# Column sums of modulation rows moved within their tiles, and identity products in two waits of TensorE at the start of the local attention

## The reference

```python
c_act = jax.nn.silu(c)
for layer in range(DEPTH):
    mod = c_act @ ada_w[layer] + ada_b[layer]
    shift, scale, gate = jnp.split(mod, 3, axis=-1)
    h = rms_norm(x, norm_w[layer]) * (1.0 + scale[:, None, :]) + shift[:, None, :]
    ...
    x = x + gate[:, None, :] * y
```

```python
sc = jnp.einsum('bnqkgd,bnskd->bnkgqs', qb, kb).astype(jnp.float32) * scale + bias
m = jnp.maximum(jnp.max(sc, axis=-1, keepdims=True), sink_l)
p = jnp.exp(sc - m)
denom = jnp.sum(p, axis=-1, keepdims=True) + jnp.exp(sink_l - m)
o = jnp.einsum('bnkgqs,bnskd->bnqkgd', (p / denom).astype(v.dtype), vb)
```

## Time and profile before

| | us |
|---|---|
| median of 3 runs | 2405.64 (2405.22 to 2407.04) |
| profiled execution: its own time | 2409.29 |
| profiled execution: span from first to last instruction | 2408.0 |
| TensorE busy | 2321.7 |
| VectorE busy | 1395.4 |
| ScalarE busy | 1133.0 |
| GpSimd busy | 929.6 |

### The profile page before, as it was taken

How to read it: one execution, slowest core, us unless ns; L and a number is a source line. 1 busy time by engine, 2 the same in 40 slices (tenths; PEclk the granted TensorE clock), 3 DMA queues, 4 the chain that set the end, 5 groups by cost and what they waited for, 6 DMA issues and landing times.

```text
span 2408.0 us, 31494 instructions
## 1 busy us (share of the span) xinstructions
PE 2321.7 (96%) x12074; PEld 1925.0 (80%) x12074; DVE 1395.4 (58%) x1899; ACT 1133.0 (47%) x1796; POOL 929.6 (39%) x711
## 2 busy tenths in 40 slices
PE   5999999999999999999999999999999999999998
PEld 5888789878888888876678868788877888888887
DVE  6255599768884320139973743332776666666665
ACT  5322388778883221249952474232333333333334
POOL 1111256447642212335521122112265555555551
PEclk9999999999999999999999999999999999999999
DMA  8255300010003221100031221121211111111111
GB/s 307 76 158 168 93 6 1 4 34 1 1 1 123 87 74 44 53 1 1 10 106 44 77 79 44 36 96 53 71 35 53 53 53 53 53 53 53 53 53 70
DMA packets 154091, 146.48 MB, mean 61 GB/s; under 512 B 12295, under 2 KB 141365, under 8 KB 152021
## 3 DMA queue, kind: packets, MB, share of 16 engines
q1 hardware_dynamic: 153940, 144.45, 19.3%
HBM read 123.85 MB, written 16.78 MB: 58 GB/s over the span
## 4 chain that ended last, share of the span: by engine, by line
PE 81%; ACT 6%; DVE 5%; issue 5%; POOL 2%; DMA 1%; SPq 0%; ACTq 0%; DVEq 0%; POOLq 0%
PE ps L256 36%; PE ps L2650 15%; PE ps L2667 9%; PE ps L1126 5%; PE ps L1149 4%; PE ps L1136 4%; ACT C_PR L1807 1%; PE ps L1696 1%; DMA MKW<-in_ada_w 1%; POOL WSL L2567 1%; ACT B_PR L1210 1%; PE ps L1675 1%; PE ps L2626 1%; ACT B_PTH L1204 1%; PE ps L1662 1%
## 5 line engine op out<-in xcount | busy, mean ns | idle before, releaser
L243 POOL TENSOR_TENSOR WL<-WR,WH 128x1024 fp32r<-128x1024 f32 (+2 forms) x87 | 203.6, 2341 | 766.1 <-ACT WH L238 765.9
L256 PE MATMUL ps<-HH,WH 128*128 128x512 f32 (+2 forms) x1136 | 358.8, 397 | 0.0
L256 PE MATMUL ps<-HL,WH 128*128 128x512 f32 (+2 forms) x1136 | 352.1, 391 | 0.0
L256 PE MATMUL ps<-HH,WL 128*128 128x512 f32 x1104 | 341.3, 391 | 0.0
L256 PEld LDWEIGHTS ps<-HL,WH 128*128 128x128 f32 (+2 forms) x1136 | 212.4, 187 | 47.8
L256 PEld LDWEIGHTS ps<-HH,WH 128*128 128x128 f32 (+2 forms) x1136 | 208.3, 187 | 46.7 <-issue 4.1
L256 PEld LDWEIGHTS ps<-HH,WL 128*128 128x128 f32 x1104 | 208.2, 189 | 44.0
L2880 DVE TENSOR_TENSOR XF<-ps,XF 128x1024 f32<-128x1024 f32 x168 | 201.5, 1220 | 32.7 <-PE ps L2667 26.1
L2650 PE MATMUL ps<-HC,WSH 128*128 128x512 f32 x640 | 197.0, 389 | 0.0
L1162 DVE TENSOR_REDUCE NM<-ps 128x1 f32<-128x1024 f32 x128 | 156.5, 1223 | 33.5 <-PE ps L1126 32.0
L2567 POOL TENSOR_TENSOR WSL<-WSR,WSH 128x512 fp32r<-128x512 f32 x100 | 131.5, 1315 | 107.6 <-ACT WSH L2561 107.6
(11 more groups left out here) (433 smaller groups left out, 5183.0 us busy)
## 6 DMA issues: line engine op xcount, KB each, us to landing
WS<-in_w_ffn_in SPq DMA_DIRECT2D x44, 512.0 KB, 5.0
MKW<-in_ada_w SPq DMA_DIRECT2D x32, 512.0 KB, 4.3
spill<-X SPq DMA_DIRECT2D x3, 4096.0 KB, 13.6
OW<-in_w_ffn_out SPq DMA_DIRECT2D x22, 512.0 KB, 3.5
WR<-in_odd_w_in SPq DMA_DIRECT2D x19, 512.0 KB, 4.0
WR<-in_w_in SPq DMA_DIRECT2D x19, 512.0 KB, 3.9
WR<-in_even_w_in SPq DMA_DIRECT2D x17, 512.0 KB, 4.2
AWK<-in_ada_w SPq DMA_DIRECT2D x8, 1024.0 KB, 9.4
```

The source lines that it names most:

```text
L243: pool.tensor_tensor(low[:, :, :], raw[:, :, :], high[:, :, :].bitcast(F32), ALU.subtract).then_inc(*w_low.up(t))
L256: last = pe.matmul(ps[0:w.out, 2 * s + h, :], wt[:, k, :], x[:, k, halves(h)], start=(k == 0 and n == 0), stop=(k == w.kt - 1 and n == len ...
```

## The change

The sums of parts 1, 2 and 3 stand after features 4, 6 and 2 of tiles 13, 15 and 17; before, they stood after feature 1 of each. Part 0 stays. In the local attention 7 identity products stand between the scores of steps 0 and 1, and 13 between the scores of step 1 and the first transposes, into bank 7.

```diff
-    MOD_SUMS = {(10, 6): 0, (13, 1): 1, (15, 1): 2, (17, 1): 3}
+    MOD_SUMS = {(10, 6): 0, (13, 4): 1, (15, 6): 2, (17, 2): 3}
...
         for u in range(NU + 4):
             if u < NU:
                 pe_c_scores(u)
-            if u == 1:
+            if u == 0:
+                pe_stay_awake(7, 7)
+            elif u == 1:
+                pe_stay_awake(13, 7)
                 pe.wait_ge(*ev_act.at(ODD_PROJ[-1]))
             if 1 <= u <= NU:
                 pe_c_turn(u - 1)
```

## The result

| | before | after |
|---|---|---|
| median of 20 runs, us | 2403.78 (2399.75 to 2409.20) | 2408.52 (2405.06 to 2410.88) |
| ratio, 95% interval | | 1.0020 (1.0013 to 1.0026) |
| profiled execution: its own time | 2409.29 | 2407.27 |
| profiled execution: span | 2408.0 | 2406.0 |

The change makes the kernel 4.7 us slower, 0.2%; 2405.4 was forecast, and 2408.52 lies outside the range. The last two lines say the opposite: of the two executions that were profiled, the one of the changed kernel is the shorter. That contradiction leads to the cause. The profiled execution of before, 2409.29, is longer than every one of its 20 runs here. Two later runs, of 2903.10 and 3857.70 us (experiments 9 and 10), lie far from the ten others of their kernels at a mean granted clock of 0.75 and 0.56, and are left out of all numbers.

What follows compares the result with a forecast made beforehand. TensorE was taken as the bound, with 6.44 us in reach at the wait before sums 2 and its low clock. The moved sums (+0.1) and identity products (-0.3) gave -0.2 us, so 2405.4 us, range 2401.3 to 2408.2.

Steps and rivals of the forecast that it cites:

- What bounds the kernel now: Even projection: TensorE's 2.91 us wait before sums 2 and the low clock after it, 6.44 us in reach.
- Part 1: Moving sums 1 to 3 later in their tiles of the even projection: +0.1 us in all.
- 3.65 over the median: Profiled execution took 2409.29 us, 3.65 over the median of 2405.64; the same difference was used to reach 2405.4.
- The rows come in time: Rival, third sums: loads near their fastest or rows ending early, the whole 6.9 us stays, 2398.5 us; 8%.
- a round of 5.78: Row loads before sums 3: each two-buffer round takes 5.78 us, 1.28 the row's own, some 4.4 the load.
- the case with loads at their fastest: Bound at sums 3: loads of 3.4 us, chain 16.7, wait 0.3, no low clock, 6.9 us earlier than now.
- Part 1, sums 1 and 2: Tiles 13 and 15: TensorE reaches sums 2 at 250.9, after the rows; wait and low clock go, gain 6.8 us.
- Part 1, sums 3: Tile 17: rows need 19.9 us, so a new 3.5 us wait, then low clock costing 2.83 + 0.70 us.
- the wait comes, the clock stays: Rival, third sums: TensorE waits 2 to 3.5 us without a low clock after it, 2401.9 us; 13%.
- Part 2: Local attention, 20 identity products: 2.1 us on the path, 2.4 us of low clock back, so -0.3 us.
- The products do not hold the clock: Rival, first six steps of local attention: thirteen products cost 2.1 us, nothing comes back, 2407.8 us; 17%.
- The signs that were named: Profile signs: no idle at sums 1, 2; 3 to 4 us at sums 3; transposes 2 us later; step 5 earlier.

Runs made afterwards that it cites:

- experiment 9: Kernel before with tile 17's weight loaded behind row 25, and 3 and 6 identity products in the local attention: 2400.81 us, ratio 0.9988.
- experiment 10: Kernel before with tile 17's weight loaded later, 3 and 6 identity products, and sums at (13, 2), (15, 3), (17, 2): 2400.43 us, ratio 0.9987.
- experiment 3: Kernel before, unchanged, measured and profiled a second time: 2403.84 us, ratio 1.0005.
- experiment 1: Kernel before with only the sums moved as in the change, no identity products: 2409.90 us, ratio 1.0020.
- experiment 7: Changed kernel with 13 identity products added before the sums of part 3: 2406.79 us, ratio 1.0010.
- experiment 6: Kernel before with the sums moved less, to (13, 2), (15, 4), (17, 3), no identity products: 2403.60 us, ratio 1.0003.
- experiment 8: Kernel before with 3 and 6 identity products in the local attention, sums not moved: 2402.87 us, ratio 0.9992.
- experiment 4: Kernel before with VectorE's row 23 made to wait for GpSimd's low half of tile 16: 2408.24 us, ratio 1.0009.

## Why the prediction was wrong, step by step

**The step that failed is the first, "What bounds the kernel now".** It took the 2.91 us of wait at sums 2 and its low clock as what the kernel pays each time, "6.44 us in reach". That is what one execution paid. In some seven of ten, by the estimate of 28%, there is nothing to win at sums 2 (experiment 3), while the new wait at sums 3 is in both profiles with the sums at the new places (after and experiment 1), and experiment 7 had to fill it. Part 1's "+0.1" is right for an execution with a late row: 95.48 against 95.37 us. For the others it is 95.37 - 89.47 = +5.9, and 0.72 x 5.9 = 4.2 us is about what was measured, 4.7 in the medians and 4.3 in the means.

The sign of it stood in the prediction itself: "3.65 over the median; the same difference from the median". The sum carried a wait with its clock of 6.4 us and the run it was read from was 3.65 us too long; the two were not put together. None of the rivals asked it either. "The rows come in time" speaks of the new place, not of the old one. The range failed with the step, since all its bounds were counted from that one execution. That 2408.52 is only 0.3 us over it is luck: the 2405.64 from which it was counted is the median of three runs, and the median of 20 is 2403.78. Two slips in its working move nothing: a round of 5.78 less the row's 1.28 leaves 4.5, not 4.4, and the case with loads at their fastest, with its wait of 0.3 us, lies 6.6 us earlier, not 6.9.

**Part 1, sums 1 and 2: right for the profiled execution.** TensorE was forecast to reach sums 2 at 250.9 and did at 250.65; no wait, no low clock. Row 23 was late there too, and took 2.55 us at 244.36, but was done 3.7 us before it was needed. This room for a late row is real, and experiment 6 shows its worth: the upper runs go.

**Part 1, sums 3: right.** 19.9 us for the chain of loads, 19.8 seen; a wait of 3.5 us, 3.38 and 3.44 seen; then the low clock of the old place, 0.60 and 0.55 over 8 us. Its price was put at 2.83 + 0.70 = 3.5 us, and experiment 7 gets 3.0 back. So "the rows come in time" (8%) and "the wait comes, the clock stays" (13%) did not happen.

**Part 2: right against the profiled execution, which was its slowest case.** Step 5 of the local attention was forecast 0.3 us earlier and came 0.39 earlier, with the loop's first scores 0.09 later. Alone, the products measure 0.9996, and the interval reaches from -0.15% to +0.07%. But the baseline was one execution here too, and of six profiles without products it is the longest: 13.34 us from the scores of step 0 to those of step 5, where the mean is 12.74 and the change takes 12.86 (experiment 8). Against the mean nothing comes back beyond what the thirteen products cost. They were too many: 3 and 6 held the clock as well and took 10.90. "The products do not hold the clock" (17%) fell: 1.00 through 1050 to 1074 and 1080 to 1130, and in all six profiles with products. So did what that rival cited from the Trainium skill, "TensorE: Matmul & The Clock Gate", section "A second HAM failure mode: psum-queue depth-cycling": in this loop TensorE stands still for 4.7 of 50 us between its groups, and the clock does not swing.

**The signs that were named.** Every one of them came out right: no idle at sums 1 and 2, 3.38 us at sums 3, 284.32 for 284.24, the transposes 2.09 us later, step 5 0.39 us earlier. They were all set against the same execution, and so could not show that it was one of the rarer kind.

## What to carry to other kernels

Before a wait in a profile is counted as a gain, compare the profiled execution's own time with the spread of the runs. If it lies near the upper end, ask whether the wait is part of the reason: search for a load that lands within a microsecond of another engine's instruction, and profile a second execution. A consumer that is moved later also moves the producer's next start; in a chain of loads that is longer than the room left for it (19.8 us here, for 12 features of 1.365), the wait then comes back one part later, as in both profiles here. Where a load decides a race, try the less urgent load behind it in the queue. Products that fill a wait should end before it does: by the profiles, 3 and 6 were better than 7 and 13.

## What was not expected of the hardware

Which of two engines begins first decides 2 us of one instruction (3.27 against 1.28) and some 6 us of the kernel (95.48 against 89.42), and a fraction of a microsecond is enough: 0.16 us behind GpSimd the row took 3.27 us, while in experiment 10, 0.12 us ahead of it, the row took 1.28 and GpSimd 3.42. The same instruction thus has two durations in two executions of one program, and the kernel's times spread over 2396.6 to 2411.0 in 34 runs.

TensorE's clock fell where it had hardly stood still. In experiment 6 the wait before sums 3 was 0.19 us, and the clock was 0.50 in the window from 272, after sums whose products have one column; in experiment 3 the same sums, after no wait, were followed by 1.00 over 272 to 280. At sums 1 it is the longer waits that kept the clock: after 0.38, 0.30 and 0.32 us (the first profile, experiments 3 and 4) it is 1.00 from 222 to 228, after 0.27 and 0.16 (experiments 8 and 9) it falls to 0.50, and the way to sums 2 takes 25.3 us instead of 23.7. That is 1.6 us of the 90.55 of experiment 8. So the length of the wait does not tell the cases apart, and what does was not tried. Nor was a third buffer for the rows, which might shorten the chain of loads itself.
